# A decoder layer with gathered experts: the shifted copy in two pieces, the block loop written out, weights in tiles of 512 columns

## The reference, cut to what matters

```
proj = rmsnorm(x) @ w_in                         # 1024 x 2816; columns 0..1791 are pa
prev = concat([last row of the block before, pa[:-1]])
xm   = pa + (prev - pa) * mu                     # token shift, feeds the RWKV heads
x   += concat(rwkv(xm), chunk_gmlp(proj)) @ w_out
q    = rmsnorm(x) @ wq                           # 8 heads x 2 x 128
eidx, gate = product-key top-16 of each head     # 128 experts per row
act  = gelu(sum(U[eidx] * x)) * gate
x   += sum(act * V[eidx])                        # rows of U and V gathered, 4 KB each
x   += (p @ ple_w) * sigmoid(rmsnorm(x) @ ple_gate_w)
```

## Time and profile before

| what | us |
|---|---|
| median of 3 runs | 4756.91 |
| lowest, highest | 4746.48, 4775.71 |
| the profiled execution | 4743.98 |
| its span, first to last instruction | 4741.9 |

### The profile page before, as it was taken

One profiled execution on the slowest core, in us unless ns is written; L12 is line 12 of the kernel. 1 busy time (PEld: TensorE's weight loads), 2 busy tenths in 40 slices (PEclk: granted clock), 3 DMA queues, 4 the chain that ended last, 5 costly groups with the idle time before them and its releaser, 6 DMA issues.

```text
span 4741.9 us, 48174 instructions
## 1 busy us (share of the span) xinstructions
PE 3170.8 (67%) x12962; PEld 2027.0 (43%) x12962; DVE 3067.9 (65%) x6057; ACT 865.7 (18%) x1858; POOL 2462.6 (52%) x2366
## 2 busy tenths in 40 slices
PE   4744676757777487657767487656867577674586
PEld 3643454335534265334644265333544355321242
DVE  1562977649584686638685486747775496857782
ACT  1210211202112211202112121212112121121112
POOL 1003765637554574546655475546655475557651
PEclk8777788878887698878888698887988798886778
DMA  4047799978989699887999699987999689998995
GB/s 147 27 153 274 275 350 337 342 249 312 350 305 359 208 336 350 312 293 269 359 333 351 216 323 354 327 311 241 348 330 342 239 320 363 322 363 313 333 332 203
DMA packets 648502, 1407.58 MB, mean 297 GB/s; under 512 B 44137, under 2 KB 369033, under 8 KB 648210
## 3 DMA queue, kind: packets, MB, share of 16 engines
q0 software_dynamic: 297216, 1082.26, 62.8%
q1 hardware_dynamic: 339010, 274.54, 18.6%
q10 hardware_dynamic: 11984, 47.40, 2.6%
HBM read 1386.84 MB, written 9.93 MB: 295 GB/s over the span
## 4 chain that ended last, share of the span: by engine, by line
PE 32%; DVE 26%; DMA 25%; issue 10%; ACT 3%; POOL 2%; ACTq 2%; another core or an unknown queue 1%; DVEq 0%; SPq 0%; PEldq 0%; POOLq 0%
DMA wbuf<-in_w_in_dram 12%; PE peer_acc L925 10%; PE bank L701 8%; DVE uring L1631 5%; DMA wbuf<-in_peer_wq_dram 4%; DMA wbuf<-in_ple_gate_w_dram 3%; DVE accv L1624 3%; DMA wbuf<-in_w_out_dram 3%; DMA xm<-proj_s 2%; PE bank L789 2%; PE bank L839 2%; ACTq L1041 2%; DVE feat L1463 1%; PE bank L837 1%; PE bank L823 1%
## 5 line engine op out<-in xcount | busy, mean ns | idle before, releaser
L629 POOL DMA_INDIRECT vring<-in_peer_v_dram,idx_c x1024 | 1172.2, 1145 | 1261.5 <-PE peer_acc L925 683.8
L925 PE MATMUL peer_acc<-vring,dg 128*128 128x512 f32 x2368 | 1280.6, 684 | 429.7 <-ACT dg L969 392.1
L619 POOL DMA_INDIRECT uring<-in_peer_u_dram,idx_c x1024 | 1145.3, 1118 | 578.2 <-issue 220.2
L1631 DVE CUSTOM_DVE_ANT_0 uring<-uring,px 128x1024 f32<-128x1024 f32 x1024 | 1243.1, 1222 | 91.6 <-DMA uring<-in_peer_u_dram,idx_c 64.2
L701 PE MATMUL bank<-wbuf,xT 128*128 128x256 f32 (+1 forms) x2736 | 797.8, 450 | 548.8 <-DMA wbuf<-in_w_in_dram 393.0
L925 PEld LDWEIGHTS peer_acc<-vring,dg 128*128 128x128 f32 x2368 | 481.3, 217 | 1023.5 <-issue 724.5
L701 PEld LDWEIGHTS bank<-wbuf,xT 128*128 128x128 f32 (+1 forms) x2736 | 564.4, 213 | 801.3 <-DMA wbuf<-in_w_in_dram 455.4
L1624 DVE SCALAR_TENSOR_TENSOR accv<-vring,pact,accv 128x1024 f32<-128x1024 f32 x424 | 544.2, 1284 | 14.3 <-issue 5.1
L1612 DVE TENSOR_TENSOR pact<-pg,pgate 128x4 f32<-128x4 f32 x256 | 40.6, 158 | 666.3 <-ACT pg L969 665.8
L789 PE MATMUL bank<-xT,wbuf 128*128 128x128 f32 (+1 forms) x2304 | 322.3, 301 | 87.3 <-DMA wbuf<-in_peer_wq_dram 73.7
L789 PEld LDWEIGHTS bank<-xT,wbuf 128*128 128x128 f32 x2304 | 317.3, 221 | 129.7 <-DMA wbuf<-in_peer_wq_dram 83.1
(11 more groups left out here) (280 smaller groups left out, 3282.7 us busy)
## 6 DMA issues: line engine op xcount, KB each, us to landing
wbuf<-in_w_in_dram SPq DMA_DIRECT2D x198, 512.0 KB, 14.0
wbuf<-in_peer_wq_dram SPq DMA_DIRECT2D x144, 512.0 KB, 12.2
wbuf<-in_w_out_dram SPq DMA_DIRECT2D x72, 512.0 KB, 10.2
wbuf<-in_ple_gate_w_dram SPq DMA_DIRECT2D x72, 512.0 KB, 10.6
uring<-in_peer_u_dram,idx_c POOLq DMA_INDIRECT x1024, 6.6
vring<-in_peer_v_dram,idx_c POOLq DMA_INDIRECT x1024, 6.6
wbuf<-in_ple_w_dram SPq DMA_DIRECT2D x18, 512.0 KB, 7.6
feat<-in_shift_mu_dram ACTq DMA_DIRECT2D x9, 896.0 KB, 10.1
```

Of the source, the lines that this page charges most:

```text
L619: gp.indirect_dma_start(uring[:, s, :], None, peer_u, bass.IndirectOffsetOnAxis(ap=idx_c[:, n % NI, j:j + 1], axis=0)).then_inc(sig(f"u{s} ...
L629: gp.indirect_dma_start(vring[:, s, :], None, peer_v, bass.IndirectOffsetOnAxis(ap=idx_c[:, n % NI, j:j + 1], axis=0)).then_inc(sig(f"v{s} ...
L925: last = mm(acc[c][:, :], dg[:, n % 2, at, :], vring[:, s, c * 512:(c + 1) * 512], start=(n + at == 0), stop=(n == UNITS - 1 and j == pe_e ...
L1631: v.tensor_tensor_reduce(out=uring[:, s, :], in0=uring[:, s, :], in1=px[:, :], scale=1.0, scalar=0.0, op0=ALU.mult, op1=ALU.add, accum_out ...
```

## The change

The token shift is copied as 112 rows and 15 rows; the row of the block before is loaded ahead of them, and the last row is stored behind them. DVE waits for three DMAs in place of two.

```
-  act.dma_start(xm[1:P, :], pa[0:P - 1, :]).then_inc(sig("prev_loaded"), 16)
-  act.dma_start(at(i + 1), pa[P - 1:P, :]).then_inc(sig("proj_stored"), 16)
   hold(sig("proj_stored"), 16 * i)
-  act.dma_start(xm[0:1, :], at(i)).then_inc(sig("prev_loaded"), 16)
+  act.dma_start(xm[0:1, :], proj_s[i:i + 1, :]).then_inc(sig("prev_loaded"), 16)
+  act.dma_start(xm[1:1 + EVEN, :], pa[0:EVEN, :]).then_inc(sig("prev_loaded"), 16)       # EVEN = 112
+  act.dma_start(xm[1 + EVEN:P, :], pa[EVEN:P - 1, :]).then_inc(sig("prev_loaded"), 16)
+  act.dma_start(proj_s[i + 1:i + 2, :], pa[P - 1:P, :]).then_inc(sig("proj_stored"), 16)
```

```
-            with eng.Fori(2, NB) as i:
+            for i in range(2, NB):
                 iteration(i, True, True)
...
-                if j == 0:
-                    copy_idx(i, n + 1)
                 gather_u(i, n + 1, j)
             gather_v(i, n, j)
```

```
+WIN_COLS = [(0, 512), (512, 512), (1024, 512), (1536, 256), (1792, 512), (2304, 512)]
+W_RING = 4
-        wbuf = sb("wbuf", [P, 2, KT * WC])
+        wbuf = sb("wbuf", [P, W_RING, 1024])
...
+                for part in range(parts_of(name)):
+                    w, used = wpart(pe, i, name, part)
+                    for kk in range(per):
+                        k = part * per + kk
+                        last = mm(b[0:n, 0:width], xT[:, k, 0:n], w[:, kk, :], start=(k == 0), stop=(k == KT - 1))
+                    if part < parts_of(name) - 1:
                         last.then_inc(used, 1)
                 filled(i, name, last)
-                pe.wait_ge(sig(f"bank{bank_of(i, name)}_filled"), count(i, name)[1] + 1)
-                pe.sem_inc(used, 1)
```

```
+            def stream_q(i, c, n):
+                b = take(pe, i, f"q{c}")
+                for part in range(4):
+                    w, used = wpart(pe, i, f"wq{c}", part)
+                    for kk in range(2):
+                        k = 2 * part + kk
+                        for r in range(4):
+                            last = mm(b[:, r * P:r * P + n], w[:, kk, r * P:(r + 1) * P], xT[:, k, 0:n], start=(k + r == 0), stop=(k == KT - 1 and r == 3))
+                    if part < 3:
+                        last.then_inc(used, 1)
+                filled(i, f"q{c}", last)
...
-                    if h < H:
+                    if h < H and h % 2 == 0:
+                        stream_q(i, h // 2, n)
                     if h:
                         keys(i, h - 1, n)
```

```
-BOTH_STAGES = (TAIL_STAGES[:TAIL_STAGES.index("gate2")] + ["norm"] + ["gate2", "gate3", "turn", "gate4", "xT", "y_norm", "y"]
+BOTH_STAGES = (TAIL_STAGES[:TAIL_STAGES.index("gate2")] + ["norm"] + ["turn", "gate2", "xT", "y_norm", "y"]
```

More of the change, by code:

```diff
@@ L343, in load_w, with chunk_use @@
-        def load_w(sp, i, name):
[L345 to L349, removed]
+        w_order = [(i, use) for i in range(NB + 3) for use in (W_TAIL if i >= 2 else []) + (W_FRONT if i <= NB else [])]
+        w_place = {use: n for n, use in enumerate(w_order)}
+        def chunk_use(name):
+            return "q" + name[2:] if name.startswith("wq") else name
@@ new lines, in w_last, with part_view, wpart, w_freed @@
+        def w_last(name, part):
+            return name == "ple" or part == parts_of(name) - 1
+        def part_view(name, ring):
+            return wbuf[:, ring, :].rearrange("p (k n) -> p k n", k=4 if name == "win3" else 2)
+        def wpart(pe, i, name, part):
+            n = w_place[i, (name, part)]
+            pe.wait_ge(sig(f"w{n % W_RING}_loaded"), 16 * (n // W_RING) + 16)
+            return part_view(name, n % W_RING), sig(f"w{n % W_RING}_used")
+        def w_freed(sp, n):
+            if n < W_RING:
+                return
+            i, (name, part) = w_order[n - W_RING]
+            if name == "ple":
+                use = f"ple{part}"
+            elif w_last(name, part):
+                use = chunk_use(name)
+            else:
+                sp.wait_ge(sig(f"w{n % W_RING}_used"), sum(not w_last(*use) for _, use in w_order[n % W_RING:n - W_RING + 1:W_RING]))
+                return
+            b, k = count(i, use)
+            sp.wait_ge(sig(f"bank{b}_filled"), k + 1)
@@ L721, in front @@
                 turn_rows(i, "xT", z, n)
-                for c in range(11):
+                for c in range(6):
                     yield f"win{c}"
@@ L766, in front @@
                 turn_rows(i, "zT", z, n)
-                for c in range(4):
+                for c in range(2):
                     yield f"wout{c}"
@@ L1181, in tail @@
                 fn(z[0:n, :], x[0:n, :], ACT.Copy, scale=st[0:n, 8:9]).then_inc(sig("t_xn_ready"), 1)
-                for c in range(4):
+                for c in range(2):
                     yield f"gate{c}"
-                    if c == 0 and (not isinstance(i, int) or i <= NB):
+                    if c == 0 and (i <= NB):
                         hold(sig("bank1_filled"), count(i, "t_xT1")[1] + 1)
                         load_x(i)
-                    evac(i, f"gate{c}", xn_gate(c)[0:n, :], WC, n, ACT.Sigmoid)
+                    evac(i, f"gate{c}", xn_gate(c)[0:n, :], 512, n, ACT.Sigmoid)
                 yield "y_norm"
@@ L1567, in take_sums @@
                 j = i - 2
[L1568 removed]
+                sample = j == NB
                 m = NS if sample else P
```

275 lines of the change are left out of this document (95 added, 180 removed).

## The result

| | before | after |
|---|---|---|
| median | 4751.69 us (4743.34 to 4775.71, 4 runs) | 4311.69 us (4298.34 to 4314.72, 4 runs) |
| span of the profiled execution | 4741.9 us | 4313.0 us |

The ratio is 0.9061, 95% interval 0.9022 to 0.9100: 440 us less by the medians, where 345 were forecast.

What follows compares the result with a forecast made beforehand. No engine is full; DMA transfers are near their limit except for a hole opened by the one-engine shifted copy. Terms 310 + 20 + 10 + 15 - 10 = 345 us off gave a forecast of 4410 us, range 4300 to 4540.

Steps and rivals of the forecast that it cites:

- shifted copy: Copy of 127 rows, on one DMA engine, split into 112 and 15: 310 us saved, bounds 200 and 350.
- loop written out: DVE's idle time at five loop turns before its px copy goes: 20 us saved, bounds 0 and 22.
- idx_c: POOL's copies of expert numbers go, relief capped by DVE in the head stage: 10 us saved in all.
- extra semaphore steps: Increments that go with the loop form, on engines said to have slack: 0 us.
- weights, tiles, norm moved: Longer weight rows gain 15 us through wq; norm behind the last gate tile loses 10; query groups of four 0.
- the second rival: Weights come sooner everywhere, longer rows getting twice the share between SP and gather queues: 4300 us, chance 0.15.
- The first (time given back): Rival: without the stall DMA may limit the head stage, blocks take 522 us: about 4545 us, chance 0.15.
- The third, lockstep: Rival: 512-column tiles delay gelu, sums and v gathers; at 3.6 us DMA idleness per tile 4810 us, chance 0.04.
- The fourth is out: Rival: the copy's 112 rows stay on one DMA engine and the hole stays: about 4720 us, chance 0.04.

Runs made afterwards that it cites:

- e1: Kernel before with only the shifted copy issued as 112 and 15 rows, ahead of the store: 4471.34 us, ratio 0.9391.
- e2: Kernel before with only the loop over blocks 2 to 7 written out: 4754.38 us, ratio 0.9984.
- e3: Kernel before with both the new shifted copy and the loop written out: 4474.00 us, ratio 0.9395.
- e4: e3 with the gathers reading eidx directly, so POOL's copies of the expert numbers go: 4388.06 us, ratio 0.9216.
- e6: e4 without the semaphore increments each engine gave itself after a wait: 4368.38 us, ratio 0.9151.
- e12: Changed kernel with PE taking each 512-column tile of w_in, w_out and gates in two steps, expert sums between: 4252.49 us, ratio 0.8927.
- e11: Changed kernel with POOL's u gathers issued two further ahead of the v gathers, six in place of four: 4311.61 us, ratio 0.9050.

## Why the prediction was right, and where its sizes were off

| term | forecast | measured |
|---|---|---|
| shifted copy | 310 | 290 (e1) |
| loop written out | 20 | none told apart (e2, e3) |
| idx_c | 10 | 85 (e3 to e4) |
| extra semaphore steps | 0 | 31 (e4 to e6) |
| weights, tiles, norm moved | 15 - 10 = 5 | 43 (e6 to after) |
| sum | 345 | 447 by the ratio |

**What held.** The hole of the 127-row copy is the change's main term, and its price, read from block 8, was good to 7% by the ratio (290 for 310; the spans of the two traces differ by 270). In those traces 34 us a block were gained for 40 in blocks 2 to 7, 38 in block 1, 40 in block 0 for 30, and 10 us were lost from block 8 on. As forecast, ACT's store no longer blocks (0.42 us; 2.07 in block 0, just over the 2 forecast), DVE's first shift step waits for no DMA but in block 0, nothing idles "issue" ahead of the px copy, and block 0 is past 26 GB/s. Px copy to last shift step came to 153 us, not 145 to 150, and blocks to 487 to 496, shorter than the 495 to 510 forecast.

**What was luck.** The sum missed by 98 us (4410 for 4312). The time lies in the range by 12 us, at an end, 4300, that the second rival had set, and that rival did not happen as told. The range's own terms did not reach so far: loop, idx_c and wq were given 0 to 100 and came, with the tiles, to 0 + 85 + 43 = 128, and the semaphore steps had no place in it.

**The first step that failed** is "POOL's relief is capped by DVE. 10 us in all". It looked at the head stage alone. The runs gain 6 us a block in the stretch before it (152.9 to 146.9), where DVE is busy half the time and the DMA engines are nearly full (0.95 in e1's window above), 3 us in the head stage, and 22 us from block 8 on. The stated bound, 22 us a block, held it, though the range of 0 to 100 for three terms had no room for that bound.

**The second** is "The register arithmetic and the extra semaphore steps go as well; they stand on engines that have slack, 0 by themselves": 20 to 31 us. On which engine they cost was not tried.

**The third** is the pair "The 8.4 MB of wq would gain 26.2 - 21.8 = 4.4 us a block" and longer tiles to which, beside the 10 for the norm, it gave no cost. The 4.4 us came from two windows of 10 us and went to wq alone. All weights gain: 882 to 772 us of engine time on q1. The queue lines of the page before held the hint, 311 GB/s for weights beside 363 for gathers, and the prediction does not use them. On the other side the longer tiles, or the groups of four with them, were no zero. Both errors were large and of opposite sign. Beside long turns rows gain some 200 us, and with short rows the rest of the edit loses some 156; counted the other way, rows and rest gain 107 us with short turns (e6 to e12), and the long turns lose 64 of them. Either way 43 is left. The norm moved behind the gate tiles was not tried by itself.

**The fourth** is "20 us, with 0 and 22 as bounds" for the loop: a wait on DVE was priced as if it ended the block; in e2 the next stretch took the time back. That transfers set the end of that stretch is the likely reason, and was not tested.

**The rivals.** The first (time given back) did not come: the head stage is 179.0 us as the table counts it, 178.1 before, and 164.36 for 164.30 in the prediction's own window. The second came nearest in time, 4300, by another road: the wait for w_in fell with the copy alone, and half of what was left did not go; the rows paid in engine time instead. Its sign, w_in landing in under 10 us, did not come (12.4, and 11.0 in e1 with short rows). Yet turns between the queues are real. On the copy's one engine, from 80 to 105 us in block 0 before, the packet records have 80 rows of the copy and 78 of w_in: one for one, and so 22.9 GB/s for rows of 7 KB beside 3.2 for rows of 1 KB. The third, lockstep, is real but not in the size that would decide: halving the tiles (9 of a block's 14) takes back 64 us, 0.6 us for each of its 112 tiles where 3.1 would have been needed. Half of its sign came, the longer wait (857.6 us), and half did not, a share under 0.9 (0.94 to 0.96). The wait was a poor sign: POOL waits longer for PE's sums even in e6 (909.2 us in its trace) without any longer tile, and 371.3 us in e11 with no gain. The fourth is out: 237 GB/s in block 0.

## What to carry to other kernels

Where the DMA engines set the pace, read each queue's line as bytes over share times span: here the queue that moved fewer GB/s than its neighbour paid for short rows, and the price fell on the whole kernel. An engine that only issues transfers was then on the path too, though it was busy only 56% of the time: a wait of 1 us ahead of every eighth gather cost 63 us. And a wider tile bought longer rows but kept in-order engines longer from everything else; the fastest run takes the pieces wide and the turns short. Edits that meet in one resource do not add: say in which order they were taken apart.

## What the runs showed of the hardware

- A copy of 127 rows kept one engine of sixteen at work (0.06 busy, 26 GB/s); 112 and 15 rows of the same data, with w_in beside them, filled all (1.01 busy, 237 GB/s), and the copy's packets took 8.7 us in place of 41.7. While the one-engine copy ran, one of ACT's next two DMAs was held in its issue for 20 to 32 us, in each of the eight blocks.
- Loads with rows of 1 KB and 512 bytes moved 311 GB/s of engine time, with rows of 2 KB 356; how many transfers bring them made no difference (4516.69 and 4517.68 us). A packet's median time was 8 ns and 38 ns per KB, from 512 bytes to 7 KB.
- One engine with rows of two queues took them in turn: 80 rows of 7 KB and 78 of 1 KB in 25 us (block 0 before).
- Not explained: without the index copies, the gathers' own engine time falls from 66.4% of 4474.1 us (2971) to 66.6% of 4385.3 (2921), though they move the same bytes. A median row of 4 KB takes 159 ns in both; the rows over 200 ns go from 6.5% to 5.3%.
